# Gate matrix of a routed layer: one fp32 product per token, or one f32r product over high and low parts

## The reference, cut to what matters

```python
sc, pos = lax.top_k(cand, PEER_TOPK)
idx = jnp.take_along_axis(cand_idx, pos, axis=-1)       # i1 * 128 + i2
g = jax.nn.softmax(sc, axis=-1).astype(t.dtype)
def block(args):
    tb, ib, gb = args
    act = jax.nn.gelu(jnp.einsum('thkd,td->thk', u[ib], tb), approximate=False)
    return jnp.einsum('thk,thkd->td', gb * act, v[ib])
```

## Time and profile before

| | us |
|---|---|
| median of the runs | 3287.16 |
| profiled execution, its own time | 3289.8 |
| its span, first to last instruction | 3288.1 |
| TensorE busy | 3202.0 (97%) |
| VectorE busy | 2126.6 (65%) |
| ScalarE busy | 1554.7 (47%) |
| 64 copies of the gate matrix, L2084, first and last start | 2148.4 and 2511.8 |

### The profile page before, as it was taken

One profiled execution on the slowest core, in us unless ns is written; L12 is line 12 of the kernel. 1 busy time (PEld: TensorE's weight loads), 2 busy tenths in 40 slices (PEclk: granted clock), 3 DMA queues, 4 the chain that ended last, 5 costly groups with the idle time before them and its releaser, 6 DMA issues.

```text
span 3288.1 us, 52008 instructions
## 1 busy us (share of the span) xinstructions
PE 3202.0 (97%) x20716; PEld 2925.6 (89%) x20716; DVE 2126.6 (65%) x3324; ACT 1554.7 (47%) x2218; POOL 29.8 (1%) x45
## 2 busy tenths in 40 slices
PE   7999998999999998999999999999999999999998
PEld 7999998999999997999999888888888888888886
DVE  3458977555555567666875779676775566666665
ACT  4454434445444446445544544544444444444444
POOL 0000000000000000000000000000000000000000
PEclk9999999999999998999999999999999999999999
DMA  9435534555555553444345566666667666666663
GB/s 285 141 129 178 181 141 143 186 185 184 189 180 187 200 189 105 151 144 152 116 180 180 189 215 203 215 208 230 220 218 291 243 244 246 246 239 245 243 218 135
DMA packets 108265, 638.86 MB, mean 194 GB/s; under 512 B 11616, under 2 KB 28160, under 8 KB 38960
## 3 DMA queue, kind: packets, MB, share of 16 engines
q1 hardware_dynamic: 100368, 591.44, 50.7%
q0 software_dynamic: 7472, 44.57, 3.9%
q10 hardware_dynamic: 240, 0.25, 0.0%
HBM read 597.42 MB, written 38.80 MB: 193 GB/s over the span
## 4 chain that ended last, share of the span: by engine, by line
PE 90%; DVE 6%; ACT 1%; DMA 1%; issue 1%; DVEq 0%; ACTq 0%; SPq 0%
PE bank L425 22%; PE bank L426 11%; PE bank L389 10%; PE bank L390 10%; PE bank L391 10%; PE bank L1124 7%; PE bank L1123 7%; PE bank L1122 7%; DVE wlo L374 2%; PE bank L1088 2%; DMA raw<-stream 1%; ACT whi L368 1%; PE bank L553 1%; PE bank L550 1%; DVE dacc L1192 1%
## 5 line engine op out<-in xcount | busy, mean ns | idle before, releaser
L374 DVE TENSOR_TENSOR wlo<-raw,whi 128x1024 fp32r<-128x1024 f32 x1056 | 1284.8, 1224 | 1064.2 <-ACT whi L368 1062.9
L368 ACT CAST whi<-raw 128x1024 fp32r<-128x1024 f32 x1056 | 1102.2, 1049 | 1155.1 <-PE bank L426 520.6
L425 PE MATMUL bank<-xboth,whi 128*128 128x512 f32 x3072 | 1089.2, 399 | 0.9 <-DVE wlo L374 0.9
L426 PE MATMUL bank<-xboth,wlo 128*128 128x256 f32 x3072 | 861.2, 280 | 0.0
L425 PEld LDWEIGHTS bank<-xboth,whi 128*128 128x128 f32 x3072 | 577.6, 188 | 137.4 <-DVE wlo L374 1.2
L426 PEld LDWEIGHTS bank<-xboth,wlo 128*128 128x128 f32 x3072 | 581.2, 189 | 0.0
L389 PE MATMUL bank<-xboth,whi 128*128 128x256 f32 x1888 | 542.0, 287 | 15.6 <-DVE wlo L374 15.6
L390 PE MATMUL bank<-xboth,whi 128*128 128x256 f32 x1888 | 536.6, 284 | 0.0
L391 PE MATMUL bank<-xboth,wlo 128*128 128x256 f32 x1888 | 536.4, 284 | 0.0
L1124 PE MATMUL bank<-wlo,aghi 128*128 128x512 f32 x1024 | 398.7, 389 | 0.0
L1122 PE MATMUL bank<-whi,aghi 128*128 128x512 f32 x1024 | 398.7, 389 | 0.0
(11 more groups left out here) (415 smaller groups left out, 3608.6 us busy)
## 6 DMA issues: line engine op xcount, KB each, us to landing
raw<-stream SPq DMA_DIRECT2D x528, 1024.0 KB, 4.8
up_activations<-ust SPq DMA_DIRECT2D x128, 128.0 KB, 5.1
gate_matrix<-gstage POOLq DMA_DIRECT2D x8, 2048.0 KB, 14.4
gslice<-gate_matrix POOLq DMA_DIRECT2D x8, 2048.0 KB, 12.3
uin<-up_activations SPq DMA_DIRECT2D x32, 512.0 KB, 5.7
relative_band<-cband POOLq DMA_DIRECT2D x1, 3072.0 KB, 36.1
xraw<-xt SPq DMA_DIRECT2D x1, 2048.0 KB, 7.7
cbias<-relative_band POOLq DMA_DIRECT2D x1, 2048.0 KB, 20.0
```

What stands on the lines that cost most here:

```text
L368: nc.scalar.copy(whi[b.half][:, k, :], raw[b.raw][:, k, :]).then_inc(hi_done, 1)
L374: nc.vector.tensor_tensor(wlo[b.half][:, k, :], raw[b.raw][:, k, :], whi[b.half][:, k, :].bitcast(f32), ALU.subtract).then_inc(lo_done, 1)
L425: nc.tensor.matmul(o[:, :], whi[b.half][:, k, :], xboth[:, :, k, :], start=k == 0, stop=False)
L426: ins = nc.tensor.matmul(o[:, 0:T], wlo[b.half][:, k, :], xhi[:, k, :], start=False, stop=k == KC - 1)
```

## The change

The four fp32 products of a group become four f32r products of 256 columns: the moving tile `one1` of a token now has 128 columns scaled by the high part of the gates and 128 scaled by the low part. The two halves of the result are added afterwards.

- VectorE's `turned_chosen` makes the high part (`gate_hi`, f32r) and the low part (`gate_lo_part`) of all gates, once.
- VectorE's `onehots(g)` makes two of the four high tiles (`TENSOR_SCALAR`, 128 columns), `one2`, and a plain one-hot tile `plain1` (one more `TENSOR_TENSOR` of 512 columns).
- ScalarE's new `scale_gates(g)`, at the end of turn n for the groups of n-1, makes the other tiles from `plain1` with 6 activations of 128 columns whose scale is a column of gates: two high ones and four low ones.
- A token has 256 columns of result, so a group fills two banks, and 2 groups instead of 4 fit into banks 4 to 7. `gate_group(g)` waits for `gate_scaled` and for the staging of the group 2 before it.
- `stage_gates(g)` moves from the end of ScalarE's turn (groups of n-2) to the start of its turn (groups of n-3), ahead of `split_hi` for block n+2. It copies the high halves in two copies of 256 columns.
- VectorE's new `add_low_gates(g)` adds the low halves, two `TENSOR_TENSOR` of 256 columns, and only then counts `stage_full`. It stands in turn n for the groups of n-3, between the two halves of `split_lo` for block n+2.

```diff
-                if g >= 4:
-                    pe.wait_ge(sem("stage_full"), g - 3)
+                pe.wait_ge(sem("gate_scaled"), g + 1)
+                if g >= 2:
+                    pe.wait_ge(sem("stage_full"), g - 1)
                 for t in range(4):
-                    ins = nc.tensor.matmul(bank(4 + g % 4)[:, 128 * t:128 * t + 128], one2[g % 4][:, t, :],
-                                           one1[g % 4][:, t, :], start=True, stop=True)
+                    ins = nc.tensor.matmul(bank(4 + 2 * (g % 2) + t // 2)[:, 256 * (t % 2):256 * (t % 2) + 256],
+                                           one2[g % 4][:, t, :], one1[g % 3][:, t, :, :], start=True, stop=True)
                 ins.then_inc(sem("gate_product"), 1)
...
             def turned_chosen():
                 dve.wait_ge(sem("chosen_turned"), 1)
-                for i in range(3):
+                for i in range(2):
                     st.link(nc.vector.tensor_copy(chosenT[i][:, :], bank(4 + i)[:, 0:T]))
+                st.link(nc.vector.tensor_copy(gate_hi[:, :], bank(6)[:, 0:T]))
+                nc.vector.tensor_tensor(gate_lo_part[:, :], bank(6)[:, 0:T], gate_hi[:, :].bitcast(f32), ALU.subtract
+                                        ).then_inc(sem("gate_parts"), 1)
...
             def onehots(g):
-                o = g % 4
-                if g >= 4:
-                    dve.wait_ge(sem("gate_product"), g - 3)
-                nc.vector.tensor_tensor(
-                    one2[o][:, :, :], iota[:, :].rearrange("p (a n) -> p a n", a=1).to_broadcast([128, 4, 128]),
-                    chosenT[1][:, 4 * g:4 * g + 4].rearrange("p (a n) -> p a n", n=1).to_broadcast([128, 4, 128]),
-                    ALU.is_equal)
-                for t in range(4):
+                if g >= 3:
+                    dve.wait_ge(sem("gate_product"), g - 2)
+                    dve.wait_ge(sem("gate_scaled"), g - 2)
+                for t in (2, 3):
                     tok = slice(4 * g + t, 4 * g + t + 1)
-                    ins = nc.vector.tensor_scalar(one1[o][:, t, :], iota[:, :], chosenT[0][:, tok],
-                                                  chosenT[2][:, tok], ALU.is_equal, ALU.mult)
+                    nc.vector.tensor_scalar(one1[g % 3][:, t, 0, :], iota[:, :], chosenT[0][:, tok],
+                                            gate_hi[:, tok].bitcast(f32), ALU.is_equal, ALU.mult)
+                for dst, row in ((one2[g % 4], chosenT[1]), (plain1[g % 3], chosenT[0])):
+                    ins = nc.vector.tensor_tensor(
+                        dst[:, :, :], iota[:, :].rearrange("p (a n) -> p a n", a=1).to_broadcast([128, 4, 128]),
+                        row[:, 4 * g:4 * g + 4].rearrange("p (a n) -> p a n", n=1).to_broadcast([128, 4, 128]),
+                        ALU.is_equal)
                 ins.then_inc(sem("onehots"), 1)
+
+            def add_low_gates(g):
+                half, i = g // 8, g % 8
+                dve.wait_ge(sem("gate_staged"), g + 1)
+                for a in range(2):
+                    rows = gstage[half % 2][:, :, 4 * i + 2 * a:4 * i + 2 * a + 2, :]
+                    low = bank(4 + 2 * (g % 2) + a)[:, :].rearrange("p (t s e i) -> p s e t i", t=2, s=2, e=SLICES)
+                    ins = nc.vector.tensor_tensor(rows, rows, low[:, 1, :, :, :], ALU.add)
+                ins.then_inc(sem("stage_full"), 1)
...
                 if n + SPLIT < 2 * CHUNKS:
-                    split_lo(dve, Block(UP + n + SPLIT))
+                    split_lo(dve, Block(UP + n + SPLIT), (0,))
+                for g in groups_at(n - 3):
+                    add_low_gates(g)
+                if n + SPLIT < 2 * CHUNKS:
+                    split_lo(dve, Block(UP + n + SPLIT), (1,))
...
+            def scale_gates(g):
+                act.wait_ge(sem("gate_parts"), 1)
+                act.wait_ge(sem("onehots"), g + 1)
+                if g >= 3:
+                    act.wait_ge(sem("gate_product"), g - 2)
+                for t in range(4):
+                    tok = slice(4 * g + t, 4 * g + t + 1)
+                    if t < 2:
+                        nc.scalar.activation(one1[g % 3][:, t, 0, :], plain1[g % 3][:, t, :], ACT.Copy,
+                                             scale=gate_hi[:, tok].bitcast(f32))
+                    ins = nc.scalar.activation(one1[g % 3][:, t, 1, :], plain1[g % 3][:, t, :], ACT.Copy,
+                                               scale=gate_lo_part[:, tok])
+                ins.then_inc(sem("gate_scaled"), 1)
+
             def stage_gates(g):
...
                 act.wait_ge(sem("gate_product"), g + 1)
-                nc.scalar.copy(gstage[half % 2][:, :, 4 * i:4 * i + 4, :],
-                               bank(4 + g % 4)[:, :].rearrange("p (t e i) -> p e t i", t=4, e=SLICES)
-                               ).then_inc(sem("stage_full"), 1)
+                for a in range(2):
+                    high = bank(4 + 2 * (g % 2) + a)[:, :].rearrange("p (t s e i) -> p s e t i", t=2, s=2, e=SLICES)
+                    ins = nc.scalar.copy(gstage[half % 2][:, :, 4 * i + 2 * a:4 * i + 2 * a + 2, :], high[:, 0, :, :, :])
+                ins.then_inc(sem("gate_staged"), 1)
             for n in range(2 * CHUNKS):
+                for g in groups_at(n - 3):
+                    stage_gates(g)
...
-                for g in groups_at(n - 2):
-                    stage_gates(g)
+                for g in groups_at(n - 1):
+                    scale_gates(g)
```

More of the change, by code:

```diff
@@ L299, in build @@
     chosenT = [ar(f"chosenT{i}", [128, T], 29 + i) for i in range(3)]
-    one1 = [ar(f"one1_{i}", [128, 4, 128], 16 + 2 * i) for i in range(4)]
-    one2 = [ar(f"one2_{i}", [128, 4, 128], 96 + 2 * i) for i in range(4)]
+    one1 = [ar(f"one1_{i}", [128, 4, 2, 128], (16, 20, 24)[i], f32r) for i in range(3)]
+    plain1 = [ar(f"plain1_{i}", [128, 4, 128], 8 + 2 * i) for i in range(3)]
+    one2 = [ar(f"one2_{i}", [128, 4, 128], 96 + 2 * i, f32r) for i in range(4)]
+    gate_hi = ar("gate_hi", [128, T], 31, f32r)
+    gate_lo_part = ar("gate_lo_part", [128, T], 14)
     gstage = [ar(f"gstage{i}", [128, SLICES, 32, 16], 64 - 16 * i) for i in range(2)]
```

## The result

The changed kernel takes 3300.45 us (median of 6 runs, 3298.16 to 3301.76), the kernel before 3287.76 (6 runs beside it, 3286.83 to 3288.59): ratio 1.0037, 95% interval 1.0027 to 1.0048. It is slower by 12.7 us; the forecast was 4.9 us faster, and the time lies above the range. The profiled execution of the changed kernel took 3299.49 us, with a span of 3297.8; the span before was 3288.1.

A forecast was written before the change was run, and what follows sets the result against it. TensorE was taken to bound the gate stage. A saving of 26.2 us less 21.3 us of new waits gave -4.9 us, from 3287.16 to 3282.3; the range was 3271 to 3296.

The forecast's parts named there:

- What TensorE saves: Gate products on TensorE: a group falls from 0.89 to 0.48 us, 26.2 us over 64 groups, or 21.1.
- the 0.08 behind it: On TensorE after a group, the next block's first product takes 0.31 us to its successor in place of 0.23.
- The 0.09 that I could not name: Unexplained difference between blocks with one group on TensorE, taken as an error of 3 us either way.
- The waits: TensorE waits for VectorE's add in the gate stage: seven of 2.37, seven of 0.43, one of 1.64; 21.3 us.
- The clock: Rival, gate stage: TensorE's clock falls in the seven long waits, 3.3 us lost each, +18, 3305; chance 8%.
- Seven waits of 2.37 us lie at the harmless end.: TensorE in the gate stage: clock stays 1.00, as after one earlier 2.4 us wait; a 3.9 us wait went with 0.67.
- The activation price: ScalarE's new scaling activation of 128 columns: 0.30 us each, 1.8 us for a group's six, ends 0.20 and 0.40.
- Cost nothing: Extra `TENSOR_TENSOR`, later last staging and slice loads, late `whi`, hidden weight loads, no added DMA: no time added.
- The upper ends: Rival, gate stage: activations at 0.40 give +4.7, 3291.9; adds at 0.59 bring 7.8 more, 3299.7; chance 13%.
- The sum: Whole kernel: -26.2 saved on TensorE + 21.3 of waits = -4.9 us, median from 3287.16 to 3282.3.

The follow-up runs named there:

- the add first: The changed kernel with VectorE's add of the low halves moved ahead of the first half of `wlo` in its turn: 3267.80 us, ratio to before 0.9934.
- the longer wait: The changed kernel with an unused ScalarE copy of 1024 columns ahead of the scaling of each pair's second group: 3309.23 us, ratio 1.0061.
- the idle fp32 products: The add first plus two unread fp32 products of 128 columns after each of up blocks 12, 58 and 117: 3263.05 us, ratio 0.9920.

## Why the prediction was wrong, point by point

- **What TensorE saves.** Forecast 26.2 us, with 21.1 as the lower bound. The stage with the add first against the stage before is 409.7 - 388.3 = 21.4 us shorter, and 23.4 once its own short waits of 2.0 are taken out. The group itself was right (0.47 to 0.48), and the 0.08 behind it did go. Of the missing 2.8 us nearly all is the rhythm: between the groups 36 of 55 blocks ran at 5.55 before and the others at 5.65, but 8 of 55 with the add first. The 0.09 that I could not name was this, and it was taken as an error of 3 us to either side; the runs show it as a loss.
- **The waits.** Forecast 21.3 us in 15 places. The profile lists 19.0 in 15 places. What they cost in the stage is 416.3 - 388.3 + 2.0 - 7.4 = 22.6: 2.36 before the second group of a pair (forecast 2.37), about 0.67 before the next group (0.43) and 1.5 once (1.64). Right in place and number, and 1.3 us too small in all.
- **The clock.** This is the step that failed: "Seven waits of 2.37 us lie at the harmless end." Five of them took the clock. The one wait of 2.4 us that had not the earlier trace rows was one sample, the rival got 8%, and it was said to decide only where a wait grows beyond 2.4 us, while waits listed as 2.1 were enough. Its price was too high as well, 3.3 where 1.5 was measured, for I took it from a window with 6.6 us at half rate, and these stretches have 3.4. The Trainium skill, page "TensorE: Matmul & The Clock Gate", section "HAM oscillation — how this bites in real kernels", describes a loop that waits for some 3 to 5 us in each turn and is throttled in each. The trace agrees that this repeats, 7 of 7 turns with waits of 3.1 us; but the waits here, at 2.1, are shorter than the page's, so the prediction carried it further than the page goes, and 5 of 7 were measured.
- **The activation price.** 0.30 by bounds, 0.29 to 0.30 in the trace. The estimate by the Trainium skill, page "ScalarE: Activation LUTs", section "What ACT_TABLE_LOAD costs", was 0.293; the duration by the same figures, also an estimate, is 0.386 where the trace has 0.393.
- **Cost nothing.** The slices of the gate matrix are loaded from 2536.5 on and first used at 2578.6, the same distance as in the earlier trace rows; nothing waits for them. Right. That the weight loads are hidden was not tested by itself.
- **The upper ends.** The price of slower adds in that rival is off by a little: 0.5 at 15 waits is 7.5 us, not 7.8, and its time 3299.4. Nothing rests on it; the adds took 0.74 us for two, as forecast.
- **The sum.** In the stage -23.4 + 22.6 + 7.4 = +6.6 us, which is 416.3 - 409.7, where -4.9 was forecast. 0.9 more come behind it, from the last blocks at 5.65 in place of 5.55. In front of it, where the code is the same, the profiled execution is 2.1 us later; half-rate stretches add up to 54.5 us there in the changed kernel, 51.1 before and 44.2 with the add first. Half of each difference, 1.7 and 3.5, is close to the distances of the starts of the up blocks, 1805.0, 1802.9 and 1799.4, but the kernel with the longer wait has as few (44.3) and starts them at 1801.7, so this is not the whole cause. The earlier start also makes up for much of the 7 us by which the add first beat its expectation. The profiles thus account for 9.7 us of the measured 12.7; the remainder is that the changed kernel's median lies 1.0 us above its profiled execution and that of before 2.0 us below its own; the cause of this is open.

Between the forecast of -4.9 us and the measured +12.7 lie 17.6 us. The clock is 7.4 of them and the largest term; the saving is 2.8 and the waits 1.3, 0.9 lie behind the stage, 2.1 in front of it, and the remaining 3 are the distances of the medians from the profiled executions. Without the 7.4 us of the clock the time would have been 3293, inside the range, which ended at 3296 because it left this rival out. The rival itself forecast 3305 by seven stretches of 3.3 us; five of 1.5 came, and that its number lies nearer to the measured one is in part luck.

## What to carry to other kernels

When a buffer is freed by one more step than before, put that step where its engine idles, ahead of work that waits for something later: here the swap of two calls was worth 33 us, 28 of them in the stage, and made a slow change the faster kernel, 20.7 us below the one before, or 25.4 with the idle fp32 products. A wait of the engine that sets the time has two prices, its length and, from some length on, slower work behind it. For products as small as these, 128 or 256 columns, count products and not columns or formats.

## What was not expected of the hardware

- A product of 128 columns, f32r or one of the two entries of an fp32 one, takes 0.11 us from start to start, one of 256 columns 0.12.
- The same f32r block of 32 products takes 5.55 or 5.65 us, and fp32 products between blocks can switch it. In one kernel two of them switched 44 blocks, 4.2 us in its profile; f32r products switched a few blocks as well, and the rule is open.
- The clock fell after waits of 2.1 us on five of seven occasions, though one wait of 2.4 us elsewhere left it; a stretch of 3.4 us at 1.2 GHz cost 1.5 us.
- A wait that the profile lists as 2.1 us cost 2.36, and one of 0.28 was not listed at all; the length from the group's first product to the next block showed both.
